# Moving the embedding gate's weights to other buffers and two earlier points, one copy order in attention, and the order of the first transposes

## The reference, cut to what matters

```python
h = _rmsnorm(x, g_mix)
u = h @ w_in                    # q, k, v of 8 forgetting heads and 4 differential heads
o_f = _fox_attention(fq, cached_and_new_k, cached_and_new_v, ...)
o_d = _rmsnorm(_diff_attention(dq, ...), diff_subln_g) * (1 - lambda_init)
x = x + concat(o_f, o_d) @ w_o
x = x + _moe(_rmsnorm(x, g_ffn), ...)              # top 4 of 32 experts, three 1024x1024 matrices each
x = x + (p_i @ w_ple_proj) * sigmoid(_rmsnorm(x, g_ple) @ w_ple_gate)
y = _rmsnorm(x, g_final)
```

## Time and profile before

| | |
|---|---|
| time of the kernel before | 1316.58 us, median of 3 runs (1314.81 to 1317.4) |
| profiled execution: its own time | 1320.0 us |
| its span, first to last instruction | 1318.2 us |
| mean granted TensorE clock | 0.970 of full speed |
| PE busy | 1206.3 us, 92% of the span |
| DMA traffic | 453.83 MB |

### The profile page before, as it was taken

The page is one execution under the profiler, slowest core; times in us unless marked ns, Lnnn a source line. Parts: engine busy times, 40 slices in busy tenths (PEclk is TensorE's granted clock), DMA queues, the critical chain, the costliest instruction groups (busy, mean ns, idle before and its releaser), DMA issues.

```text
span 1318.2 us, 15815 instructions
## 1 busy us (share of the span) xinstructions
PE 1206.3 (92%) x5925; PEld 500.8 (38%) x5925; DVE 313.2 (24%) x880; ACT 180.5 (14%) x416; POOL 75.7 (6%) x143
## 2 busy tenths in 40 slices
PE   5999978989999999999899889999988989988866
PEld 4665656443333333333333333333323333333322
DVE  2343555252211211111111111211111111111253
ACT  2223333010100000000100000010000010000122
POOL 6000011000000000000000000000000000000000
PEclk9999986979999999999999999999999999999988
DMA  9551155379999988999999999979999999999761
GB/s 292 195 160 32 52 193 201 131 285 375 404 429 427 430 358 371 428 431 427 428 429 429 428 426 429 419 317 428 428 428 428 428 428 430 428 427 427 287 234 40
DMA packets 63940, 453.83 MB, mean 344 GB/s; under 512 B 9089, under 2 KB 26089, under 8 KB 39333
## 3 DMA queue, kind: packets, MB, share of 16 engines
q1 hardware_dynamic: 57712, 442.26, 81.6%
q0 software_dynamic: 4128, 10.78, 2.2%
q10 hardware_dynamic: 2068, 0.37, 0.2%
HBM read 444.16 MB, written 14.47 MB: 348 GB/s over the span
## 4 chain that ended last, share of the span: by engine, by line
PE 55%; DMA 39%; DVE 2%; ACT 2%; issue 1%; SPq 1%; POOL 0%; ACTq 0%; POOLq 0%; DVEq 0%
PE ps L813 51%; DMA ring<-in_w_up 37%; DMA ring<-expert_rows 1%; PE ps L825 1%; PE ps L1072 1%; SPq L477 1%; ACT area L732 1%; DVE X L1643 0%; DMA X<-in_x_sample 0%; PE ps L922 0%; PE ps L924 0%; ACT H L615 0%; PE ps L953 0%; DVE area L1279 0%; ACT ring L665 0%
## 5 line engine op out<-in xcount | busy, mean ns | idle before, releaser
L813 PE MATMUL ps<-ring,area 128*64 128x512 f32 x3232 | 722.9, 596 | 58.3 <-DMA ring<-in_w_up 46.3
L813 PEld LDWEIGHTS ps<-ring,area 128*64 128x64 f32 x3232 | 224.4, 137 | 509.8 <-issue 397.9
L813 PE MATMUL ps<-ring,hT 128*128 128x512 f32 (+2 forms) x320 | 111.3, 571 | 6.0 <-DMA ring<-in_w_ple_gate 4.6
L1508 DVE TENSOR_SCALAR area<-ps 128x512 f32<-128x512 f32 x32 | 22.1, 692 | 367.6 <-PE ps L813 367.6
L813 PE MATMUL ps<-H,area 128*64 128x512 f32 (+1 forms) x420 | 103.4, 610 | 1.1 <-DVE area L1483 1.1
L586 POOL DMA_INDIRECT expert_rows<-area,rowi x34 | 33.1, 974 | 939.9 <-ACT area L737 939.9
L813 PE MATMUL ps<-area 128*64 128x1 f32 (+7 forms) x756 | 80.8, 292 | 1.7 <-issue 1.2
L1514 DVE TENSOR_SCALAR area<-ps 128x512 f32<-128x512 f32 x34 | 23.5, 691 | 239.1 <-PE ps L813 230.0
L813 PE MATMUL ps<-hT,ring 128*128 128x320 f32 x256 | 75.3, 450 | 0.0
L813 PEld LDWEIGHTS ps<-ring,hT 128*128 128x128 f32 (+1 forms) x320 | 46.8, 175 | 65.2 <-issue 60.6
L722 ACT ACTIVATE area<-ps 128x512 f32<-128x512 f32 x35 | 20.9, 597 | 338.8 <-PE ps L813 338.8
(11 more groups left out here) (216 smaller groups left out, 572.8 us busy)
## 6 DMA issues: line engine op xcount, KB each, us to landing
ring<-in_w_up SPq DMA_DIRECT2D x64, 2048.0 KB, 25.8
ring<-in_w_down SPq DMA_DIRECT2D x64, 2048.0 KB, 22.3
ring<-in_w_gate SPq DMA_DIRECT2D x62, 2048.0 KB, 24.4
ring<-in_w_in SPq DMA_DIRECT2D x16, 512.0 KB, 8.4
ring<-in_w_in SPq DMA_DIRECT2D x2, 2048.0 KB, 9.7
ring<-in_w_o SPq DMA_DIRECT2D x2, 2048.0 KB, 15.3
early<-in_w_gate SPq DMA_DIRECT2D x2, 2048.0 KB, 19.1
ring<-expert_rows SPq DMA_DIRECT2D x8, 512.0 KB, 11.4
```

The lines of the kernel that those rows point to most:

```text
L813: return T.matmul(out, lhsT, rhs, start=first, stop=last)
L1508: V.tensor_scalar(gate, ps[:, b, :], LIMIT, None, ALU.min).then_inc(g_sb, 1)
```

## The change

The gate weights get a new home, `early`, and are loaded in two halves of 2 MB, each issued by SP in the middle of its work for one of the two doubles; what was in `early` at the end (p, `gfin`, `wproj`, their products) goes to ring slots 0 and 1. SP's loop over the experts is cut in three for this. The small tail loads wait for the last expert's piece 0 to be used, where before they waited for an early piece of item 1. In attention ACT copies the first transposed weights of the last pair ahead of `exponents(14)`, and DVE's normalization of the differential rows moves from behind pair 6 to behind pair 7. At the front, PE transposes the forgetting heads' cached keys first, then the rows of x with banks 4 to 7 first, then the other cached keys.

```diff
-        wple = ring[:, 0:2, :].rearrange("p b n -> p (b n)").rearrange("p (c n) -> p c n", c=DC)
-        late = early[:, :, :].rearrange("p b n -> p (b n)")
-        ple = late[:, 0:NT * D].rearrange("p (t n) -> p t n", t=NT)
...
+        wple = early[:, :, :].rearrange("p b n -> p (b n)").rearrange("p (c n) -> p c n", c=DC)
+        wproj = ring[:, 0, 0:2048].rearrange("p (c n) -> p c n", c=2)
+        prow = ring[:, 0, 2048:2816].rearrange("p (t n) -> p t n", t=NT)
+        gfin = ring[:, 0, 2816:3840]
+        ple = ring[:, 1, 0:NT * D].rearrange("p (t n) -> p t n", t=NT)
+        pT = ring[:, 1, 3072:3712].rearrange("p (c n) -> p c n", c=2)
...
+        kc_in = [sem("kc_in0"), sem("kc_in1")]
...
-            with sp.Fori(1, NE - 3) as j:
-                e = loaded((j, 1))
+            def load_around(i, between=None):
+
+                e = loaded(item(i, 1))
                 for s in range(2, PPI):
-                    wait_used((j, 0), s)
+                    if s == 4 and between is not None:
+                        sp.dma_start(wple[:, between * 4:between * 4 + 4, :],
+                                     w_gate_rows[:, between * 4:between * 4 + 4, :]).then_inc(tail_in[0], 16)
+                    wait_used(i, s)
                     load(e, s)
...
+            with sp.Fori(1, DOUBLES[0]) as j:
+                load_around((j, 0))
+            load_around((None, DOUBLES[0]), 0)
+            with sp.Fori(DOUBLES[0] + 1, DOUBLES[1]) as j:
+                load_around((j, 0))
+            load_around((None, DOUBLES[1]), 1)
+            with sp.Fori(DOUBLES[1] + 1, NE - 3) as j:
+                load_around((j, 0))
...
-            sp.wait_ge(ahead[1], 16)
-            wait_used(SECOND, 1)
+            wait_used((nl, 0), 0)
             sp.dma_start(prow[:, 0:2, :], ...
...
-            wait_used((nl, 0), 1)
...
-                if t == 0:
-                    sp.dma_start(wple, A["w_ple_gate"][0].rearrange("(c p) n -> p c n", p=P)).then_inc(tail_in[0], 16)
...
-                for c in range(DC):
-                    act_e.wait_ge(hT_ps, DC * k + c + 1)
+                for j, c in enumerate((4, 5, 6, 7, 0, 1, 2, 3)):
+                    act_e.wait_ge(hT_ps, DC * k + j + 1)
...
+                last = p == PAIRS - 1
-                if p < PAIRS:
+                if p < PAIRS and not last:
                     exponents(2 * p)
...
                     evac_PT(o)
+                    if j == 0 and last:
+                        exponents(2 * p)
                     if j == 0 and p < PAIRS:
                         exponents(2 * p + 1)
...
-            pe.wait_ge(rows_ok, NT)
-            rows_to_T(0, range(DC), lambda c: pe.wait_ge(gT_sb, 1) if c == 7 else None)
-
-            pe.wait_ge(kc_in, 32)
-            for x in range(2):
+            def cached_keys(x, guard):
+
+                pe.wait_ge(kc_in[x], 16)
                 for m in range(4):
-                    pe.wait_ge(hT_sb, 4 * x + m + 1)
+                    guard(m)
...
+            cached_keys(0, lambda m: None)
+            pe.wait_ge(rows_ok, NT)
+            pe.wait_ge(gT_sb, 1)
+            rows_to_T(0, (4, 5, 6, 7, 0, 1, 2, 3), lambda c: pe.wait_ge(kc_sb, c + 1) if c < 4 else None)
+            cached_keys(1, lambda m: pe.wait_ge(hT_sb, m + 1))
+            pe.wait_ge(hT_sb, DC)
...
-                    pe.wait_ge(tail_in[0], 16)
+                    pe.wait_ge(tail_in[0], 32)
...
-                if p == 6:
+                if p == 7:
                     dve.wait_ge(sub_rstd, NT)
```

More of the change, by code:

```diff
@@ L244, in build @@
         rscr = nc.dram_tensor("rel_by_distance", [DH, P, 769], F32, kind="Internal").ap()
-        x_in, g_in, small_in, kc_in, vc_in, ff_in, tab_in = [sem(n) for n in ("x_in", "g_in", "small_in", "kc_in", "vc_in", "ff_in", "tab_in")]
+        x_in, g_in, small_in, vc_in, ff_in, tab_in = [sem(n) for n in ("x_in", "g_in", "small_in", "vc_in", "ff_in", "tab_in")]
+        kc_in = [sem("kc_in0"), sem("kc_in1")]
         bias_in, bias_part, rel_out, rel_rows, rel_in, out_dma = [sem(n) for n in ("bias_in", "bias_part", "rel_out", "rel_rows", "rel_in", "out_dma")]
@@ L366, in _ @@
             for x, n in enumerate(("cache_fox_k", "cache_diff_k")):
-                sp.dma_start(kcache[x], A[n].rearrange(RE[n], p=P)).then_inc(kc_in, 16)
+                sp.dma_start(kcache[x], A[n].rearrange(RE[n], p=P)).then_inc(kc_in[x], 16)
             sp.dma_start(wff[:, :, :], w_in[:, :, OFF_FF:OFF_FF + FH]).then_inc(ff_in, 16)
@@ L443, in loaded @@
                 return sp.value_load(loadtab[0:1, bass.ds(lin(i, 1), 1)], min_val=0, max_val=NE - 1)
-            with sp.Fori(1, NE - 3) as j:
-                e = loaded((j, 1))
+            def load_around(i, between=None):
+                e = loaded(item(i, 1))
                 for s in range(2, PPI):
-                    wait_used((j, 0), s)
+                    if s == 4 and between is not None:
+                        sp.dma_start(wple[:, between * 4:between * 4 + 4, :],
+                                     w_gate_rows[:, between * 4:between * 4 + 4, :]).then_inc(tail_in[0], 16)
+                    wait_used(i, s)
                     load(e, s)
-                e = loaded((j, 2))
+                e = loaded(item(i, 2))
                 for s in range(2):
-                    wait_used((j, 1), s)
+                    wait_used(item(i, 1), s)
                     load(e, s)
+            w_gate_rows = A["w_ple_gate"][0].rearrange("(c p) n -> p c n", p=P)
+            with sp.Fori(1, DOUBLES[0]) as j:
[6 more added lines that the diff above has]
+                load_around((j, 0))
             e = loaded((None, NE - 2))
```

## The result

The kernel after takes 1310.86 us, the median of 14 runs. The kernel before, run beside it, takes 1317.35 us (14 runs, 1313.96 to 1322.3, mean 1317.8). The ratio is 0.9942 [0.9929, 0.9956]: faster by 0.44 to 0.71%, or 7.6 us (5.8 to 9.4). The forecast was 1310.1, and 6.5 us.

The account below looks back on a forecast made before the run. Weight transfers were taken to bound most of the expert loop, PE or a short PE, ACT and DVE chain the parts around it. 0 + 4.7 + 0.8 + 1.0 = 6.5 us off 1316.6 gave 1310.1, range 1305.5 to 1313.5.

Parts of the forecast that it names:

- The halves cost 0: Expert loop: gate-weight halves fit gaps in the transfer stream, cost 0; without that cover 9.8 us by rate.
- The tail, 4.7 us: Behind the loop: tile 1 half 0 starts at 1280.15 instead of 1284.89, gaining 4.7 us; bounds 2.3 and 4.9.
- All three waits: PE in the tail: 2.3 us for gate weights, idle 1.75 ahead of tile 1's transposes, idle 0.85 for its copy.
- the 9.9 kept: Tail: the first gate product, tile 0 half 0, was assumed to take 9.9 us as before, part at half clock.
- The upper bound of 4.9: Tail: most that could be gained, 4.9 us, if all three PE waits went in full.
- The last pair, 0.8 us: End of attention: ACT's 0.84 us wait for PE's transposes goes, gaining 0.8 us; bounds 2 gained, 1.6 lost.
- slow clock in the key transposes: Last pair, loss bound: half clock through most of the 24 key transposes, 5.5 us instead of 4.07, 1.6 us lost.
- The front, 1.0 us: Kernel start: forgetting heads' keys transposed first bring the forget product earlier, gaining 1.0 us; bounds 1.3 lost, 4.4 gained.
- Forget product at 26.2: Front: PE's forget product was to start at 26.2 us, where it started at 27.17 before.
- The rival with 4.4: Front: the clock rises early with PE busy from 11.2, gaining 4.4 us instead of 1.0, total 1306.7; chance 0.18.
- both earlier parts lose: Rival: front -1.3 and last pair -1.6 with the tail's 4.7, sum 1.8 us, total 1314.8; chance 0.08.
- The sum, 6.5 us: Whole kernel: halves 0, tail 4.7, last pair 0.8 and front 1.0 make 6.5 us off, 0.5% faster.

Follow-up runs that it names:

- e1_tail: Kernel after with the front's order, the last pair's copy order and DVE's normalization put back as before; 1314.4 us against 1316.92, ratio 0.9967.
- e3_pair7: Kernel before with only the last pair's new copy order and the normalization moved behind pair 7; 1317.83 us against 1316.92, ratio 1.0002.
- e2_front: Kernel before with only the new order of the first transposes; 1314.23 us against 1316.92, ratio 0.9978.
- e4_full_stream: Kernel after with the two gate halves issued at items 13 and 25, in the full stream, instead of at the doubles; 1318.51 us against 1316.92, ratio 1.0016.
- e8_norm_early: Kernel after with DVE's normalization left behind pair 6; 1308.36 us against 1317.66, ratio 0.9934.
- e6: Kernel after with extra unread products where PE waits for ACT in and behind pair 7; 1298.89 us against 1317.66, ratio 0.9858.
- e7: Kernel after with 14 extra unread products ahead of the tail's first transposes and 9 behind them; 1304.46 us against 1317.66, ratio 0.9908.
- e9: Kernel after with the added products of e5, e6 and e7 together; 1297.29 us against 1319.01, ratio 0.9835.
- e10: Kernel before, old order of first transposes, with 24 extra unread products at the front; 1318.64 us against 1319.01, ratio 0.9994.
- e5: Kernel after with 12 extra unread products ahead of the transpose of the gains and 12 behind it; 1307.11 us against 1317.66, ratio 0.9926.

## Why the prediction was right, and where it was not

Four positions of PE in profiled executions (us), all ahead of the expert loop; "order" is that of the first transposes, "copies" that of ACT's copies in the last pair:

| | order, copies | first projections end | last scores end | third values start | loop starts |
|---|---|---|---|---|---|
| before | old, old | 44.0 | 191.2 | 203.0 | 308.6 |
| e1_tail | old, old | 42.7 | 190.9 | 202.7 | 308.0 |
| e3_pair7 | old, new | 46.3 | 193.5 | 204.1 | 309.4 |
| e2_front | new, old | 39.4 | 186.5 | 198.4 | 304.0 |
| after | new, new | 45.2 | 193.3 | 203.9 | 308.6 |
| e4_full_stream | new, new | 44.8 | 192.1 | 202.7 | 308.4 |
| e8_norm_early | new, new | 39.8 | 187.1 | 197.7 | 303.7 |

- *The halves cost 0*: right. 0.06 us in the trace, less than the stretch varies, and 10.15 without the gaps (e4; forecast 9.8). The places, near 478 and at the second double, and the rate in the gaps (298 and 296 GB/s, two thirds of the loop's) are as written. The pieces behind the first half are issued at 497.56, before at 497.63.
- *The tail, 4.7 us*: right in mechanism, the size 1.3 too small in the trace. All three waits went. Tile 1 starts earlier than worked out, since the product for tile 0's first half took 9.29 us and not the 9.9 kept, and since the transposes and products behind it run without gaps. The upper bound of 4.9 held the starts to waits alone and left out the pace, so it was too low. On average over runs (e1) the tail is worth 4.3, between 2.5 and 6.2, so over runs the 4.7 isn't refuted.
- *The last pair, 0.8 us*: the wait that went is the one named, and 1.26 us are gained up to the third values in every trace (11.81 to 11.84 us from the scores' end with the old copy order in four traces, 10.55 or 10.56 with the new one in six). What the forecast held as a bound, slow clock in the key transposes, isn't what decides: they vary from 3.85 to 4.75 us, but the way from the third values to the loop is 104.9 to 105.6 us with the old order of copies and 104.8 to 106.0 with the new. In the total the gain doesn't show (e3), at most 1.6 us, since the clock's course ahead of it varies by more.
- *The front, 1.0 us*: this is the step that was mis-sized. "Forget product at 26.2" was right to a tenth, but the gain was read off its start, with its 5.37 us kept. At the slow pace it takes 8.77, and PE is through with it 2.3 us later than before; 1.2 of these remain behind the first projections (45.2 against 44.0). In another execution of the same order (e2) the clock rises early and 4.6 us are gained. And the old order has no fixed end either: 42.7, 44.0 and 46.3 in three traces. So the difference between two single executions sizes the course of the clock more than the new order; the mean over runs is 2.9 (0.7 to 5.1). The rival with 4.4 had been given 0.18; it is the course of the profiled executions of e2, e6, e7 and e8, while after and e4 have the late one.
- *One bound doesn't follow from its numbers*: in the last pair key transposes of 5.5 for 4.07 us cost 1.4, which with the 0.8 gained makes 0.6 lost and not 1.6. The rival "both earlier parts lose" then sums to 4.7 - 1.3 - 0.6 = 2.8, or 1313.8, and not 1314.8. The forecast itself doesn't change.
- *The sum, 6.5 us*: by the ratio 7.6 (5.8 to 9.4), so it was near and a little low. It is right in part by luck, since the terms err both ways: in the pair of profiled executions it is 6.0 for the tail and about 0 for the rest, where 4.7 and 1.8 were forecast; by the parts' own ratios it is 4.3 + 2.9 - 0.3 = 6.9.

The kernel after has times in two groups, 1304.8 to 1308.7 (seven runs) and 1313.0 to 1314.6 (six), some 6 us apart. The profiled execution of the upper group shows the late clock at the front. That of e8, at 1309.14, with the same instructions there, shows the early one, with the loop 4.95 us earlier (303.65 against 308.60); from the loop's start to the end the two spans are equal, 1003.7 us. This fits in size, but isn't shown for each run, and e1 has two groups with the old front. There the second place comes in. From the end of the first projections to that of the last scores it is 147.2 to 147.3 us in eight profiled executions, 148.1 or 148.2 in two (after, e1) and 144.2 in two (e9, e10). The Trainium skill, TensorE: Matmul & The Clock Gate, "Part 1: The HAM clock gate", says that the stretch at the lower clock at a kernel's start varies between runs of one kernel; the two courses of the same instructions agree. Products ahead of the first keys brought the early course in the one execution that was profiled (e5), though one of its six runs was still 5 us above the rest. What decides an execution's course without them stays open.

## What to carry to other kernels

Look in the loop for the places where the stream runs dry because a buffer is held longer, and put transfers of later stages there: 4.2 MB were free in them and cost 10 us elsewhere. When a step is moved, cost what follows it at both clock levels until PE has been seen at full pace again, and not its start alone. Before a microsecond is read off two traces, see how much the same stretch differs between traces of kernels that share its code: here it was up to 4 us. And read what PE does behind an idle time of some microseconds: if the granted clock is 0.50 there, products that nobody reads may be worth more in that idle time than any reordering. The pace was up behind them where real work followed within 1.7 us (e5, e6, e7), and not where 3.5 us of idle time did (e10).

## What the runs showed of the hardware that was not expected

- Filling the 5.3 us of idle time in pair 7 and the 0.95 us waits behind it gained nothing up to the third values and 9.1 us at the loop's start (e6 against e8). With them unfilled TensorE was at 0.50 for most of the 30 us up to the output projection.
- At the span's start the clock column reads 1.00 while the pace is that of 0.50: sixteen key transposes in 3.67 us there, 1.97 with the clock up. There the pace of equal instructions tells the clock, and the column does not.
- The same 24 row transposes take 7.38 us at a granted 0.50 and 4.66 at 1.00, a factor of 1.58 and not 2: not all of an instruction follows the clock.
- Two executions with the same instructions at the front differed by 5 us in where the first projections end (45.2 in the kernel after, 39.8 in e8), and the stretch behind that, up to the last scores, took from 144.2 to 148.2 us with the same instructions on PE.
